# Banded attention scores contracted over 64 partitions, two heads at a time, on the two halves of the TensorE array

## What is computed

```python
A_HEADS = 16; A_KV_HEADS = 4; A_GROUP = 4; A_HEAD_DIM = 64; WINDOW = 128; BLK = 128
q = q.reshape(B, nb, BLK, A_KV_HEADS, A_GROUP, A_HEAD_DIM) * (A_HEAD_DIM ** -0.5)
kb = _band(k...)          # for each block of 128 queries: the key blocks before, at and after it
scores = einsum('bnqkgd,bnskd->bnkgqs', q, kb)
scores = scores - slopes * dist                 # ALiBi, then the mask |t-s| <= 128
p = softmax(concatenate([scores, sink_col]))[..., :-1]
out = einsum('bnkgqs,bnskd->bnqkgd', p, vb)
```

## Time and profile before

| | |
|---|---|
| three timed runs | 1266.66, 1268.41, 1269.77 us; median 1268.41 |
| profiled execution | 1270.9 us; its span 1268.9 us, so 2.0 us lie around the span |
| mean granted TensorE clock | 0.985 of full speed |
| banded attention | about 61 to 200 us of the span |
| busy in the span | PE 95%, PEld 79%, DVE 50%, POOL 33%, ACT 29% |

### The profile page before, as it was taken

How to read it: one execution, slowest core, us unless ns; L and a number is a source line. 1 busy time by engine, 2 the same in 40 slices (tenths; PEclk the granted TensorE clock), 3 DMA queues, 4 the chain that set the end, 5 groups by cost and what they waited for, 6 DMA issues and landing times.

```text
span 1268.9 us, 19233 instructions
## 1 busy us (share of the span) xinstructions
PE 1200.9 (95%) x5796; PEld 996.9 (79%) x5796; DVE 632.2 (50%) x1051; ACT 371.3 (29%) x723; POOL 421.5 (33%) x467
## 2 busy tenths in 40 slices
PE   6988899999999999999989899999999999999996
PEld 5777787878888888888967677778788888888885
DVE  5667665443433534445476767745433332343432
ACT  4267662222210011111265666632222200111101
POOL 3355543333321332234142313215333321333342
PEclk8899999999999999999999999999999999999998
DMA  6211012323333233332201001013323432333331
GB/s 158 67 34 33 17 34 67 95 87 99 103 105 91 83 99 98 98 113 88 76 17 36 19 17 33 1 34 116 100 83 99 118 92 83 91 97 99 111 88 66
DMA packets 176471, 96.61 MB, mean 76 GB/s; under 512 B 8752, under 2 KB 173104, under 8 KB 176432
## 3 DMA queue, kind: packets, MB, share of 16 engines
q1 hardware_dynamic: 176432, 96.12, 26.1%
HBM read 94.01 MB, written 2.10 MB: 76 GB/s over the span
## 4 chain that ended last, share of the span: by engine, by line
PE 80%; DVE 7%; issue 5%; ACT 3%; POOL 3%; DMA 1%; DVEq 0%; ACTq 0%; POOLq 0%; SPq 0%
PE bank L986 25%; PE bank L988 25%; PE bank L987 25%; PE bank L1428 2%; POOL w_hi L441 1%; PE bank L1125 1%; DVE w_lo L1510 1%; DVE stat L2034 1%; POOL bias L515 1%; DVE bpt_lo L2039 1%; DMA x_n<-in_x 1%; DVE apt_lo L1696 0%; ACT s_b L917 0%; DVE k_dup L1616 0%; DVE w_lo L1527 0%
## 5 line engine op out<-in xcount | busy, mean ns | idle before, releaser
L1510 DVE TENSOR_TENSOR w_lo<-w_raw,w_hi 128x1024 fp32r<-128x1024 f32 (+2 forms) x151 | 202.5, 1341 | 299.0 <-POOL w_hi L441 298.9
L441 POOL TENSOR_SCALAR w_hi<-w_raw 128x1024 fp32r<-128x1024 f32 (+3 forms) x159 | 183.5, 1155 | 422.0 <-PE bank L988 411.1
L986 PE MATMUL bank<-x_hi,w_lo 128*128 128x512 f32 x784 | 309.5, 395 | 10.1 <-DVE w_lo L1510 7.9
L987 PE MATMUL bank<-x_lo,w_hi 128*128 128x512 f32 x784 | 307.8, 393 | 0.0
L988 PE MATMUL bank<-x_hi,w_hi 128*128 128x512 f32 x784 | 307.7, 393 | 0.0
L986 PEld LDWEIGHTS bank<-x_hi,w_lo 128*128 128x128 f32 x784 | 148.6, 189 | 42.5 <-DVE w_lo L1510 5.8
L988 PEld LDWEIGHTS bank<-x_hi,w_hi 128*128 128x128 f32 x784 | 148.7, 190 | 31.6
L987 PEld LDWEIGHTS bank<-x_lo,w_hi 128*128 128x128 f32 x784 | 148.7, 190 | 29.7
L986 PE MATMUL bank<-f_hi,w_lo 128*128 128x512 f32 x352 | 137.8, 391 | 1.0 <-DVE f_lo L1806 1.0
L988 PE MATMUL bank<-f_hi,w_hi 128*128 128x512 f32 x352 | 137.0, 389 | 0.0
L987 PE MATMUL bank<-f_lo,w_hi 128*128 128x512 f32 x352 | 137.0, 389 | 0.0
(11 more groups left out here) (222 smaller groups left out, 1916.2 us busy)
## 6 DMA issues: line engine op xcount, KB each, us to landing
w_raw<-in_ffn_w_gu SPq DMA_DIRECT2D x88, 512.0 KB, 3.8
w_raw<-in_ffn_w_down SPq DMA_DIRECT2D x32, 704.0 KB, 4.4
w_raw<-in_a_w_qkv SPq DMA_DIRECT2D x12, 512.0 KB, 3.7
w_raw<-in_a_w_o SPq DMA_DIRECT2D x8, 512.0 KB, 3.6
w_raw<-in_b_w_o SPq DMA_DIRECT2D x8, 512.0 KB, 3.7
w_raw<-in_b_w_in SPq DMA_DIRECT2D x4, 672.0 KB, 4.1
w_raw<-in_b_w_uq SPq DMA_DIRECT2D x4, 576.0 KB, 4.0
x_n<-in_x SPq DMA_DIRECT2D x4, 512.0 KB, 5.4
```

Of the source, the lines that this page charges most:

```text
L441: pool.tensor_scalar(split_part(w_hi, s, cols, kv), raw_part(s, cols, kv), 1.0, 1.0, ALU.mult, ALU.mult) \
L986: pe.matmul(o, ll, rh, start=start, stop=False)
L987: pe.matmul(o, lh, rl, start=False, stop=False)
L1510: dve.tensor_tensor(split_part(w_lo, s, cols, kv), raw_part(s, cols, kv), f(split_part(w_hi, s, cols, kv)), ALU.subtract) \
```

## The change

`scores(u)` becomes `score_pair(u)`, called for every even u. It issues the six matmuls of two heads in turn, lower half and upper half, each over 64 partitions only; zeros are no longer read. The `s_done` counts come at the end of the six. The pair waits once, until the reader of unit u-2 is through (an `s_free` count of u-1 in the group), since its second head writes the bank that unit u-2 held. Before, only the odd unit of a pair waited for that, and the even one for the reader of u-3.

```diff
-                def scores(u):
-                    n, hd = u // HG, u % HG
+                def score_pair(u):
+                    n, i = u // HG, u % HG // 2
                     k0, nk = A_KB[n]
 
-                    before = 16 * g + (u - 2 if u >= 3 else (0, -2, -1)[u])
+                    before = 16 * g + (u - 1 if u >= 2 else 0)
                     pe.wait_ge(s_free, S_A + before)
-                    q = (slice(None), hd // 2, slice(n * P, (n + 1) * P))
-                    k = (slice(None), hd % 2, slice(k0 * P, (k0 + nk) * P))
-                    product(banks[u % 3][:, 0:nk * P], aq_hi[q], aq_lo[q], kp_hi[k], kp_lo[k], True, True) \
-                        .then_inc(s_done, 1)
+                    for wl, wh in ((False, True), (True, False), (False, False)):
+                        for b in range(2):
+                            rows = slice(b * HD, (b + 1) * HD)
+                            q = (aq_lo if wh else aq_hi)[rows, i, n * P:(n + 1) * P]
+                            k = (kp_lo if wl else kp_hi)[rows, b, k0 * P:(k0 + nk) * P]
+                            ins = pe.matmul(banks[(u + b) % 3][:, 0:nk * P], q, k, start=wh, stop=not (wl or wh))
+                            if not (wl or wh):
+                                ins.then_inc(s_done, 1)
...
-                scores(0)
-                scores(1)
+                score_pair(0)
...
-                        scores(4 * n + 4)
-                        scores(4 * n + 5)
+                        score_pair(4 * n + 4)
                         if n == 0:
                             next_q((3,))
-                        scores(4 * n + 6)
-                        scores(4 * n + 7)
+                        score_pair(4 * n + 6)
```

More of the change, by code:

```diff
@@ L1170, in a_group @@
                 pe.wait_ge(q_ready, 2 * g + 2)
-                scores(2)
-                scores(3)
+                score_pair(2)
                 for n in range(NT):
```

## The result

The changed kernel took 1274.37 us at the median of 20 runs (1269.42 to 1276.20), the kernel before 1269.05 us at the median of 20 (1265.46 to 1270.94). The ratio of the two sets of runs is 1.0039, 95% interval 1.0029 to 1.0050 (it is not the quotient of the two medians, which is 1.0042): slower by about 5 us. The forecast was 1269.4 us, with a range from 1266.5 to 1273.0 us. The profiled execution of the changed kernel took 1273.96 us with a span of 1271.8 us and a mean granted clock of 0.979; before it was 0.985.

The account below looks back on a forecast made before the run. In the banded attention, scores were taken to wait for their consumers, with a fixed chain behind unit 12. Terms of 0.7 + 0.3 + 0 = 1.0 us on 1268.4 gave 1269.4 us, range 1266.5 to 1273.0 us.

Parts of the forecast that it names:

- the chain behind the read of unit 12: Fixed dependent steps from the read of unit 12 to `transposes(2, 1)`, 3.33 us in each group.
- unit 12's delay by order: Unit 12 complete only with the fifth matmul: later by 0.18 us in (b), 0.24 in (c), nothing in (a), per group.
- case (c): Array halves take turns, each matmul costing 0.12 or 0.18 us as before; sum 2.2 us, 1270.6 us; chance 0.24.
- the three cases: How the two array halves go together in a pair: full overlap, loads one behind the other, or taking turns.
- (b): Matmuls of a pair overlap but weight loads follow one another, 0.10 us each; sum 1.0 us; chance 0.33, the one taken.
- (a): Both halves run at once, a pair takes as long as one unit did; sum 0, 1268.4 us; chance 0.22.
- the three terms: Unit 12 later, pair 10 and 11 longer, pair 14 and 15 longer: 0.7, 0.3 and 0 us in (b).
- I take no net change: Slow-clock stretches, 0.7 us each, may come in four groups or none, 1.4 us either way; priced at no change.
- the emptied array: Rival: changing between 128 and 64 rows empties the array, 0.27 to 0.45 us each, up to 1273.9 us; chance 0.15.
- the ten places: Row changes on the path: before unit 12 and behind pair 14 in four groups, behind pair 10 in two slow-clock groups.

Follow-up runs that it names:

- changed and filled kernel: Changed kernel plus six idle matmuls of 512 columns over 128 partitions ahead of units 10 and 11 in each group; 1266.09 us, ratio 0.9989 to the kernel before.
- the run with half rows at the old idle time: Kernel before with score matmuls over 64 partitions, one head after the other, order and waits of before; ratio 1.0052 to the kernel before.
- the run with the idle time alone: Kernel before, 128 partitions and old order, only unit 10 waits for the reader of unit 8 like unit 11; ratio 1.0030 to the kernel before.
- the kernel before and filled: Kernel before plus the same six idle matmuls over 128 partitions between units 10 and 11; 1267.95 us, ratio 1.0001 to the kernel before.

## Why the prediction was wrong

The bound was read rightly: nothing was gained from faster scores, the chain behind the read of unit 12 was unchanged (113.48 - 110.14 = 3.34 us in the changed and filled kernel against 3.33), and unit 12's delay by order came out at 0.24 us with full rows, as the case (c) had it.

Between the three cases the choice was wrong. The forecast took (b), loads one behind the other, from a row of loads over 128 rows. The array does (a): a pair took the time of one unit, 0.12 and 0.18 us a step. The Trainium skill (TensorE: Matmul & The Clock Gate, Part 3) had that right for this pair, and the trace agrees. That made the sum of the three terms too large, not too small, in a kernel that came out slower: in (a) it is nothing.

The step that failed is the clock, "I take no net change", with 1.4 us either way. The measured 1274.37 us lies 5.0 us over the forecast. The step failed twice. The forecast knew that (a) makes the idle time 2.5 us long (it was 2.62), but it let idle time alone decide, and so expected two more falls at the most. The clock fell in all four groups of the kept execution, and the run with half rows at the old idle time shows that the rows alone can do that (ratio 1.0052); the run with the idle time alone shows that it costs something too (1.0030). And it priced a fall at 0.7 us, from falls that began after the wait and lasted 3.4 us. In the first three groups after the change the fall begins during the wait, lasts for nearly 7 us and costs 2.1 us each (8.72 - 6.64 in the second); in the last it costs 1.0 us. That is 7.2 us where four falls at 0.7 us are 2.8.

The rival on the other side, the emptied array, had the sign for another reason. Its price was put at 0.27 to 0.45 us for each change; it is 0.18 us going in and 0.19 us going back, and of the ten places only the four in front of unit 12 count, 0.8 us, with 0.2 us between reads 0 and 8 of the last group that no term had. The Trainium skill (TensorEngine Tiling (Array Packing), Key Properties) says that a change of tiling mode drains TensorE; these rows, with a pause of 0.18 to 0.19 us at each change, agree.

Not settled: why work over 64 rows ahead of a wait lets the clock fall more often and for longer; the runs show that it does, and not why. Nor how much of the 5 us each of the two, longer idle time and half rows, carries when they come together. Alone they gave ratios of 1.0030 and 1.0052, and they don't add. Nor is it explained why the changed and filled kernel came out 0.1% under the kernel before and filled, although its groups are 0.8 us longer; differences of the clock ahead of the attention, as in the two rows from 40 to 57 us, are as large as that.

## What to carry to other kernels

Matmuls over 64 partitions on the two halves of the array ran at once here and nearly halved the time of the stream (two in each step of 0.12 us). Look first at whether anything waits for that stream: where TensorE waits for its consumers, as here, the saved time becomes idle time, and what it costs is read from the granted clock behind the next wait. If a wait of 2 us can't be avoided, move useful full-row work of TensorE into it, and compare the clock's stretches before comparing busy times.

## What was not expected of the hardware

- Two matmuls of 64 rows, each with its own load of 128 columns, start together and take 0.28 us for 256 columns, as one does; the loads too overlap.
- The same stream over 64 rows instead of 128, with the same 2.03 us of idle time behind it, had the granted clock at its lower level for nearly 7 us in three groups of four (0.81, 0.50, 0.55 in three stretches of 3 us in the second). Over 128 rows, even with 2.62 us of idle time, the falls in the kept execution lasted about 3.4 us (1.00, 0.63, 0.80 and 0.93, 0.50, 1.00). The rows left out held zeros in the keys.
- Going from matmuls over 128 rows to ones over 64 cost 0.18 us, and going back 0.19 us.
- Adding 1.4 us of matmuls to each group of the changed kernel, whose results nobody reads, took 0.5% off its time.
